# RMS norms of a 512-token network: the sums and the inverse root taken with tokens on the partitions

## What is computed

```python
def rmsnorm(x, g):
    xf = x.astype(jnp.float32)
    y = xf * lax.rsqrt(jnp.mean(xf * xf, axis=-1, keepdims=True) + EPS)
    return (y * g.astype(jnp.float32)).astype(x.dtype)
...
x = x + jnp.concatenate([mix, mem_o], axis=-1) @ w_out
x = x + conv_glu_ffn(rmsnorm(x, g_ffn[i]), f_w_up[i], f_conv_w[i], f_conv_b[i], f_w_down[i])
...
h = modulate(rmsnorm_2(x, g_pre1[l]), sh1, sc1)     # h * (1 + sc1) + sh1
...
x = x + gt1 * rmsnorm_2(y, g_post1[l])
```

## Time and profile before

| | us |
|---|---|
| median of 3 runs | 2332.74 |
| lowest and highest run | 2330.17, 2342.95 |
| the profiled execution, first to last instruction (span) | 2328.2 |
| PE busy | 2129.7 |
| DVE busy | 1305.7 |
| POOL busy | 736.1 |
| ACT busy | 693.4 |

### The profile page before, as it was taken

One profiled execution on the slowest core, in us unless ns is written; L12 is line 12 of the kernel. 1 busy time (PEld: TensorE's weight loads), 2 busy tenths in 40 slices (PEclk: granted clock), 3 DMA queues, 4 the chain that ended last, 5 costly groups with the idle time before them and its releaser, 6 DMA issues.

```text
span 2328.2 us, 25743 instructions
## 1 busy us (share of the span) xinstructions
PE 2129.7 (91%) x9632; PEld 1646.4 (71%) x9632; DVE 1305.7 (56%) x2164; ACT 693.4 (30%) x1099; POOL 736.1 (32%) x181
## 2 busy tenths in 40 slices
PE   6889989899999977898999999679999987999996
PEld 4765567688778864566888888467776665888885
DVE  5878886633953776767336435374433357322336
ACT  4312364322122124552221222223434313212221
POOL 2422102344434431113344443121211232444432
PEclk8989799999999988899999999699999998999998
DMA  4221001422532521003325323121111121223221
GB/s 166 91 73 54 23 1 46 140 102 83 204 135 79 183 94 45 24 24 108 125 74 206 109 87 106 61 79 66 38 55 37 55 91 53 92 75 115 92 83 68
DMA packets 31485, 200.18 MB, mean 86 GB/s; under 512 B 3488, under 2 KB 3616, under 8 KB 13344
## 3 DMA queue, kind: packets, MB, share of 16 engines
q1 hardware_dynamic: 26496, 164.64, 20.6%
q10 hardware_dynamic: 4896, 34.30, 3.9%
HBM read 196.82 MB, written 2.10 MB: 85 GB/s over the span
## 4 chain that ended last, share of the span: by engine, by line
PE 50%; DVE 5%; ACT 1%; issue 0%; POOL 0%; ACTq 0%; DVEq 0%
PE psum L1253 42%; PE psum L1379 2%; PE psum L1410 2%; PE psum L1275 1%; PE psum L1625 1%; DVE work L889 1%; PE psum L1392 1%; DVE work L868 1%; PE psum L1356 1%; DVE h_lo L872 1%; DVE xT L884 0%; DVE work L878 0%; DVE work L893 0%; DVE stats L940 0%; PE psum L1612 0%
## 5 line engine op out<-in xcount | busy, mean ns | idle before, releaser
L509 POOL TENSOR_TENSOR w_lo<-raw,w_hi 128x2048 fp32r<-128x2048 f32 (+2 forms) x176 | 735.7, 4181 | 1561.0 <-ACT w_hi L526 1561.0
L1253 PE MATMUL psum<-h_hi,w_hi 128*128 128x512 f32 x1560 | 623.7, 400 | 11.6 <-POOL w_lo L509 10.1
L1253 PE MATMUL psum<-h_lo,w_hi 128*128 128x512 f32 x1560 | 619.0, 397 | 0.0
L1253 PE MATMUL psum<-h_hi,w_lo 128*128 128x512 f32 x1560 | 618.7, 397 | 0.0
L526 ACT ACTIVATE w_hi<-raw 128x2048 fp32r<-128x2048 f32 (+2 forms) x176 | 301.0, 1710 | 585.4 <-PE psum L1253 479.0
L1253 PEld LDWEIGHTS psum<-h_hi,w_hi 128*128 128x128 f32 x1560 | 297.9, 191 | 91.1 <-issue 20.1
L1253 PEld LDWEIGHTS psum<-h_hi,w_lo 128*128 128x128 f32 x1560 | 297.4, 191 | 74.1 <-issue 12.6
L1253 PEld LDWEIGHTS psum<-h_lo,w_hi 128*128 128x128 f32 x1560 | 298.1, 191 | 72.0 <-issue 12.7
L1253 PE MATMUL psum<-g_hi,w_hi 128*128 128x512 f32 x528 | 206.6, 391 | 8.0 <-issue 5.0
L1253 PE MATMUL psum<-g_hi,w_lo 128*128 128x512 f32 x528 | 205.5, 389 | 0.0
L1253 PE MATMUL psum<-g_lo,w_hi 128*128 128x512 f32 x528 | 205.5, 389 | 0.0
(11 more groups left out here) (240 smaller groups left out, 2710.4 us busy)
## 6 DMA issues: line engine op xcount, KB each, us to landing
raw<-w_up SPq DMA_DIRECT2D x66, 1024.0 KB, 4.8
raw<-w_dn SPq DMA_DIRECT2D x48, 704.0 KB, 4.0
mod_w<-w_mod ACTq DMA_DIRECT2D x24, 1024.0 KB, 5.6
raw<-w_c_in SPq DMA_DIRECT2D x13, 1024.0 KB, 4.9
raw<-w_a_in SPq DMA_DIRECT2D x11, 1024.0 KB, 4.9
raw<-w_b_in SPq DMA_DIRECT2D x7, 1024.0 KB, 4.8
raw<-w_a_out SPq DMA_DIRECT2D x8, 640.0 KB, 3.9
raw<-w_b_out SPq DMA_DIRECT2D x8, 640.0 KB, 3.9
```

The costliest lines, as they stand in the source:

```text
L509: nc.gpsimd.tensor_tensor(LO[slot][:, 0:ph.size], RAW[slot][:, 0:ph.size], HI[slot][:, 0:ph.size].bitcast(F32), ALU.subtract).then_inc(lo_ ...
L1253: ins = nc.tensor.matmul(out, l, r, start=(k == 0 and m == 0), stop=(k == n - 1 and m == 2))
```

## The change

In eleven of the twelve norms (all but ckv) the operands of the summing matmuls change places: 128 tokens of squares are the stationary operand and one column of the ones matrix is the moving one, so the sums of 128 tokens land on 128 partitions in one column. A norm of 512 tokens has 4 such tiles, and each one is a matmul with its own weight load. The root and the reciprocal are then 128x4 (128x2 for 256 tokens), into the new tiles `ROOT` and `INV`. PE lays the inverse out again: for every tile of tokens the column of `INV`, broadcast to 128 columns, is the stationary operand and the identity is the moving one, which leaves the inverse of all tokens on all partitions in bank 4 (bank 3 for mem). DVE's scaling reads it from PSUM in place of `T[:, 3]`. Two semaphores are added, `inverse_ready` (DVE to PE) and `inverse_spread` (PE to DVE). Norms that are not in `SPREAD` keep the sums of the tiles in four banks, 4 to 7. Bank 4 now stays taken until the last chunk has been scaled: `last_read[4]` becomes `scaled_ready` or `x_ready` in place of `root_ready`.

```diff
--- before.py
+++ after.py
@@ -301,6 +301,7 @@
         CST, PRM, ONES = after("const", [NCONST]), after("params", [NPARAM]), after("ones", [P])
         MODV, DER = after("mod", [48, 2]), after("derived", [5, 8])
         ST, M8, WARM = after("stats", [2, 12]), after("top8", [8]), after("tables_warm", [16])
+        ROOT, INV = after("roots", [ROWT]), after("inverses", [ROWT])
 
         CKX, CVX = at("ctx_k", 32, [MEM]), at("ctx_v", 33, [2, P])
         CK, CV = at("c_k", 34, [S]), at("c_v", 52, [ROWT, P])
@@ -342,15 +343,29 @@
                 ("mem", 8, MEM, True), ("mix0", 8, S, True), ("ckv", 2, S, True), ("ffn0", 8, S, True),
                 ("mix1", 8, S, True), ("ffn1", 8, S, True), ("final", 8, S, False), ("ctx", 8, MEM, True),
                 ("pre1", 8, S, True), ("post1", 8, S, False), ("pre2", 8, S, True), ("post2", 8, S, False)]):
-            NORMS[name] = (i, nch, rows, nb, sc)
+            NORMS[name] = (i, nch, rows, nb, sc if splits else None)
             nb += 1 if name in SPREAD else nch
             sc += nch if splits else 0
         square_ready, square_used, root_ready = sem("square_ready"), sem("square_used"), sem("root_ready")
         sum_ready = sem("sum_ready")
+        inverse_ready, inverse_spread = sem("inverse_ready"), sem("inverse_spread")
         scaled_ready, h_hi_ready, h_ready = sem("scaled_ready"), sem("h_hi_ready"), sem("h_ready")
         x_ready = sem("x_ready")
         XR = {"final": 0, "post1": 8, "post2": 16}
 
+
+        def token_sums(name):
+
+            n = NORMS[name][2] // P
+            if name in SPREAD:
+                return bank(4, 0, n)
+            return ps[:, 4 * S:8 * S].rearrange("p (t n) -> p t n", n=S)[:, 0:n, 0]
+
+        ORDER_N = list(NORMS)
+
+        def spread_count(name):
+
+            return sum(n != "ckv" for n in ORDER_N[:ORDER_N.index(name) + 1])
 
         steps, flushes = [], []
 
@@ -559,7 +574,11 @@
 
                     nc.scalar.activation(WARM[:, i:i + 1], cst("eps"), ACT.Sqrt)
                 act.wait_ge(square_used, b + (1 if name in SPREAD else nch))
-                nc.scalar.activation(T[:, 2, 0:rows], bank(4, 0, rows), ACT.Sqrt, bias=cst("eps"),
+                if name == "ckv":
+                    dst_r, sums = T[:, 2, :], bank(4)
+                else:
+                    dst_r, sums = ROOT[:, 0:rows // P], token_sums(name)
+                nc.scalar.activation(dst_r, sums, ACT.Sqrt, bias=cst("eps"),
                                      scale=1.0 / width).then_inc(root_ready, 1)
                 if after_root:
                     after_root()
@@ -865,7 +884,13 @@
             def norm(name, src, gain, shift=None, dst=(HH, HL), into=None):
                 i, nch, rows, b, s = NORMS[name]
                 v.wait_ge(root_ready, i + 1)
-                step(nc.vector.reciprocal(T[:, 3, 0:rows], T[:, 2, 0:rows]))
+                if name == "ckv":
+                    step(nc.vector.reciprocal(T[:, 3, 0:rows], T[:, 2, 0:rows]))
+                    inv = T[:, 3, 0:rows]
+                else:
+                    nc.vector.reciprocal(INV[:, 0:rows // P], ROOT[:, 0:rows // P]).then_inc(inverse_ready, 1)
+                    v.wait_ge(inverse_spread, spread_count(name))
+                    inv = bank(3 if name == "mem" else 4, 0, rows)
 
                 def low(k):
                     v.wait_ge(h_hi_ready, s + k + 1)
@@ -875,7 +900,7 @@
                 for k in range(nch):
                     if into is not None:
                         out = src(k) if into == "self" else T[:, 4 + k % 2, 0:rows]
-                        ins = nc.vector.scalar_tensor_tensor(out=out, in0=src(k), scalar=gain(k), in1=T[:, 3, 0:rows],
+                        ins = nc.vector.scalar_tensor_tensor(out=out, in0=src(k), scalar=gain(k), in1=inv,
                                                              op0=ALU.mult, op1=ALU.mult)
                         if into == "self":
                             ins.then_inc(x_ready, 1)
@@ -886,7 +911,7 @@
                     t = T[:, 4 + k % 2, 0:rows]
                     if k >= 2:
                         v.wait_ge(h_ready, s + k - 1)
-                    ins = nc.vector.scalar_tensor_tensor(out=t, in0=src(k), scalar=gain(k), in1=T[:, 3, 0:rows],
+                    ins = nc.vector.scalar_tensor_tensor(out=t, in0=src(k), scalar=gain(k), in1=inv,
                                                          op0=ALU.mult, op1=ALU.mult)
                     if shift is not None:
                         step(ins)
@@ -1346,16 +1371,45 @@
             def norm(name):
                 i, nch, rows, b, s = NORMS[name]
                 bank_free(4)
+                if name == "ckv":
+                    for k in range(nch):
+                        pe.wait_ge(square_ready, b + k + 1)
+                        nc.tensor.matmul(bank(4, 0, rows), ONES[:], T[:, k % 2, 0:rows], start=(k == 0),
+                                         stop=(k == nch - 1)).then_inc(square_used, 1)
+                    last_read[4] = (root_ready, i + 1)
+                    return
+                tiles = range(rows // P)
                 if name in SPREAD:
                     pe.wait_ge(sum_ready, SPREAD.index(name) + 1)
-                    nc.tensor.matmul(bank(4), ONES[:], T[:, 3, :], start=True, stop=False)
                     pe.wait_ge(square_ready, b + 1)
-                    nc.tensor.matmul(bank(4), ONES[:], T[:, 1, :], start=False, stop=True).then_inc(square_used, 1)
-                for k in range(0 if name in SPREAD else nch):
-                    pe.wait_ge(square_ready, b + k + 1)
-                    nc.tensor.matmul(bank(4, 0, rows), ONES[:], T[:, k % 2, 0:rows], start=(k == 0),
-                                     stop=(k == nch - 1)).then_inc(square_used, 1)
-                last_read[4] = (root_ready, i + 1)
+                    for t in tiles:
+                        nc.tensor.matmul(bank(4, t, t + 1), T[:, 3, t * P:(t + 1) * P], ONES[:, 0:1], start=True, stop=False)
+                        ins = nc.tensor.matmul(bank(4, t, t + 1), T[:, 1, t * P:(t + 1) * P], ONES[:, 0:1], start=False, stop=True)
+                    ins.then_inc(square_used, 1)
+                else:
+                    for t in tiles[1:]:
+                        bank_free(4 + t)
+                    for k in range(nch):
+                        pe.wait_ge(square_ready, b + k + 1)
+                        for t in tiles:
+                            ins = nc.tensor.matmul(bank(4 + t, 0, 1), T[:, k % 2, t * P:(t + 1) * P], ONES[:, 0:1],
+                                                   start=(k == 0), stop=(k == nch - 1))
+                        ins.then_inc(square_used, 1)
+                    for t in tiles[1:]:
+                        last_read[4 + t] = (root_ready, i + 1)
+                pe.wait_ge(inverse_ready, spread_count(name))
+                b = 4
+                if name == "mem":
+                    b = 3
+                    last_read[4] = (root_ready, i + 1)
+                for t in tiles:
+                    ins = nc.tensor.matmul(bank(b, t * P, (t + 1) * P), INV[:, t:t + 1].broadcast_to([P, P]), cst("ident", P),
+                                           start=True, stop=True)
+                ins.then_inc(inverse_spread, 1)
+                if s is not None:
+                    last_read[b] = (scaled_ready, s + nch)
+                else:
+                    last_read[4] = (x_ready, XR[name] + nch)
 
             def h_chunk(name):
                 s = NORMS[name][4]
@@ -1527,7 +1581,7 @@
                 unit_ready(ph, u)
                 b = (u % 2) * 2
                 if u == 1:
-                    last_read[4] = (root_ready, NORMS["mix1"][0] + 1)
+                    last_read[4] = (scaled_ready, NORMS["mix1"][4] + DC)
                     advance(r_tiles(ph, u, range(4), range(4, 8), 0, 256))
                     for t in range(4):
                         last_read[4 + t] = (qkv_ready, 11 + t + 1)
@@ -1578,7 +1632,7 @@
                 if u == 2:
                     advance(t_tiles(ph, u, (0,), (0,)))
                     last_read[0] = (ph.free, 5)
-                    last_read[4] = (root_ready, NORMS["pre1"][0] + 1)
+                    last_read[4] = (scaled_ready, NORMS["pre1"][4] + DC)
                     advance(r_tiles(ph, u, range(4), range(4, 8), P, P))
                     for t in range(4):
                         last_read[4 + t] = (qkv_ready, 17 + t + 1)
```

## The result

The changed kernel takes 2365.27 us (median of 4 runs, 2357.30 to 2371.16) where the kernel before took 2331.45 beside it (2322.94 to 2342.95). The recorded ratio, which is not simply that of the medians, is 1.0123, interval 1.008 to 1.0165. By the medians the change costs 34 us. The forecast was +8.8, and the new median lies above the prediction's range, which ended at 2356. The profiled execution took 2360.68 us, its span is 2358.6, 30.4 more than before; its granted clock has a mean of 0.933, where before had 0.947.

A forecast was written before the change was run, and what follows sets the result against it. PE was taken as the bound, busy 2129.7 of 2328.2 us. Terms -2.1 - 0.3 - 3.0 + 2.95 + 9.65 + 1.6 = +8.8 us gave a median of 2341.5, range 2327 to 2356.

The forecast's parts named there:

- largest term: Between post1 and pre2: the held bank 4 delays pre2's sums until post1's last addition, +9.65 us.
- same: Whole kernel: time within 0.5% or 11.7 us of the kernel before; chance 0.58.
- Passes: Norm sums: one moving column is spaced as 128 are, 0.11 us at clock 1.00 and 0.21 at 0.50.
- rival 2: Every sum and inverse: passes spaced by the load's whole record, 0.33 us at 0.50; +33.5, 2375 us; chance 0.10.
- pre1: Norm pre1: all sums at clock 0.50 make the root 3.9 us later; net +2.95 us.
- rival 1: Norm sums: the clock comes up and passes take 0.11 us; sum -5.5, time 2327.3 us; chance 0.15.
- post1 and pre2: pre2's sums wait for bank 4 until post1's last addition; root +10.6, less 0.95, net +9.65 us.
- Root to PE: Wait from root to PE's restart: 7.3 us for 9.2 in ffn0, 9.1 for 10.05 in pre1.
- rival 4: ffn0, mix1, ffn1: chunk 0's h_lo gets in before POOL's pass, 10 us won, 2332 us; chance 0.05.
- the SPREAD norms at clock 1.00: SPREAD norms: 16 passes behind the last square add 0.85 us, and the inverse takes 1.25, at clock 1.00.
- rival 3: Behind the norms the clock stays low longer; half of ten resumptions give +8.5, 2350 us; chance 0.14.
- The start: Start, with mem and mix0: later weight copy and colder PE against faster scalings, net +1.6 us, from -1.6 to +5.

The follow-up runs named there:

- w_wide_ones: warm_index with 128 columns of ones instead of one in the sums of mem, mix0, ctx, pre1 and pre2: 2324.90 us, ratio 0.9932.
- own_bank: The changed kernel with post1's inverse moved to bank 3: 2350.12 us, ratio 1.007.
- w_late_split: w_spread_only with the second weight copy and POOL's split in ffn0, mix1 and ffn1 behind the first two copies of h: 2320.90 us.
- w_best: w_spread_only with the seven-chunk sums of the SPREAD norms ahead of the wait for the last squares: 2309.95 us, ratio 0.9883.
- w_best_wide: w_best with 128 columns of ones as moving operand in the six SPREAD norms: 2307.53 us, ratio 0.9876.
- w_spread_only: warm_index with the old norm in mem, mix0, ctx, pre1 and pre2, and post1's inverse in bank 3: 2320.71 us, ratio 0.9903.
- start_old: The changed kernel with the old sums and reciprocal in mem and mix0: 2350.30 us, ratio 1.0069.
- w_all_wide: warm_index with post1's inverse in bank 3, seven-chunk sums ahead of the last wait, and 128 columns of ones everywhere: 2310.36 us, ratio 0.9879.
- warm_index: The changed kernel with 32 unused 512-column matmuls while PE waits for the first index queries: 2340.69 us, ratio 1.0025.
- again: The changed kernel run and profiled once more without any edit: 2355.93 us, ratio 1.012.

## Why the prediction was wrong

The direction of its sum was right, and so was its largest term; its size was not, and the "same" that it gave the best chance did not come. By its own steps:

- **Passes.** 64 in 13.9 us at 0.50 were forecast, 13.81 and 13.78 measured. One moving column is spaced as 128 are: rival 2 falls. The forecast that narrow sums do not raise the clock held in pre1 and pre2, against rival 1. The Trainium skill (TensorE: Matmul & The Clock Gate, What's actually happening) has activity release the throttle; the trace does not agree for these passes, with PE busy for 13.8 us at 0.50, and agrees for the 128-column ones of w_wide_ones.
- **pre1.** +3.2 for +2.95. **post1 and pre2.** +11.2 for +9.65, by the mechanism named; own_bank shows 9.0 of it. The rest is post1, which was to end 1.5 earlier and ended 0.4 later (see the step that failed).
- **Root to PE.** 7.34 and 8.84 us for 7.3 and 9.1; POOL's cover is as forecast, rival 4 falls, and w_late_split shows what it hides.
- **The step that failed: the SPREAD norms at clock 1.00.** I priced 16 passes at +0.85 and the inverse at 1.25 us, "at 1.00". The clock falls in this place: in ffn0, final, post1 and post2 it drops within the 16 passes. From the start of the last square to the root (us, the profiles of before and after):

| | ffn0 | mix1 | ffn1 | final | post1 | post2 |
|---|---|---|---|---|---|---|
| before | 1.91 | 2.86 | 1.91 | 1.91 | 1.91 | 1.91 |
| after | 4.04 | 4.42 | 2.79 | 3.92 | 3.83 | 3.50 |
| difference | +2.1 | +1.6 | +0.9 | +2.0 | +1.9 | +1.6 |
| forecast | +0.85 | +1.6 | +0.85 | +0.85 | +0.85 | +0.85 |

The lines of post2 before, and in the changed kernel:

```profile
2308.55 0.69 DVE L993 TENSOR_TENSOR work<-y 128x512 f32<-128x512 f32 x1
...
2310.46 0.69 ACT L562 ACTIVATE work<-psum,const 128x512 f32<-128x512 f32 x1 [14.64 <-PE psum L1353]
```

```profile
2338.90 0.69 DVE L1018 TENSOR_TENSOR work<-y 128x512 f32<-128x512 f32 x1
...
2342.40 0.26 ACT L581 ACTIVATE roots<-psum,const 128x4 f32<-128x4 f32 x1 [16.22 <-PE psum L1387]
...
2342.93 2.08 PE L1406 MATMUL psum<-const,inverses 128*128 128x128 f32 x8 [0.57 <-DVE inverses L891]
```

The inverse takes 2.08. So from the root to the first scaling there are 2.64 us for 4.11, a gain of 1.47 where 2.35 were forecast, and the late root eats it. ffn0 +0.1, ffn1 -0.5, final with ctx 0 and post2 +0.1 stand for -5.1 in all, and post1's share is the same miss. w_best and w_best_wide, which differ only in the width of the sums, show that the one-column passes are what lets the clock fall ahead of the inverse. Where the clock stayed up through the sums, the sum's price was right (ffn1, +0.9), but the gain was not whole: PE restarts 1.0 us sooner against its last square in ffn1, and then runs at 0.50 for 4.4 us of its products where it was 3.4 before, so that 0.5 is left. That is the mechanism of rival 3. ffn0 of w_spread_only, with its sums at 1.00 too, brought 0.8 of the forecast 1.05. The earlier trace rows already showed PE idle for 1.48 us ahead of these passes; I took their price from rows of a busy PE.

- **The start.** +2.6 for +1.6, within its bounds. But start_old and w_spread_only, which have the old norms there, keep 1.3 and 1.1 of the loss, so the nearness is partly luck.
- **c_out, +1.5, had no term.** A stretch of 3.4 us at 0.50 (1886.8 to 1890.2 in the changed kernel) stands there, and none before. It is in every trace with one-column sums in pre1, but also in two with wide ones (c_out 45.4 in w_wide_ones and in w_all_wide) and in w_late_split, which has the old ones. The cause is open.
- **The index stage had no term either**, and needed a wider range instead. Its draw gives 11.8 of the 30.4 us between the profiles. It was in sight beforehand: three runs of the same kernel lay 13 us apart.

The sum on a steady clock is 19.1 us, itself with 1.1 of an untouched piece; the medians of the first comparison lie 34 apart. I put the other 15 down to draws of the index stage: the traces have it from 128 to 149 us long, and warm_index, without it, is 15 below again. For single unprofiled runs this is argued, not shown.

## What to carry to other kernels

Before a result is moved into a bank that is read later than before, list who needs that bank next: here one chunk loop's worth of cover (9 us) hung on it, and a spare bank gave it back. Price small matmuls that follow a wait at the low clock, put those that need not wait ahead of the wait, and don't take a one-column matmul for the cheaper one: here it cost as much as 128 columns and left the clock down. When runs of one kernel scatter by more than the effect, find the stage that scatters and steady it first.

## What the runs showed of the hardware that was not expected

- A dense run of fp32 passes with one moving column kept the clock at 0.50 for all of its 13.8 us, in pre1 and pre2 of every trace that has one there; with 128 columns it came up after 29 passes in pre1 and 21 in pre2 of w_wide_ones. The cost of a pass did not depend on the width: 0.213 us at 0.50 and 0.112 at 1.00 for both.
- After one wait of 7 us the index stage ran at 0.50 for 15.4, 15.5, 47.7 or 51.2 us with PE busy throughout (the last in own_bank):

```profile
151.50:202.70 51.20, 51.20 (x100) 28.35 (x100) 17.18 (x30) 7.16 (x15) 4.59 (x1) 0.50 0.12 41
```

The same program showed the first and the third. Filling the wait with 7.42 us of unused matmuls took 15 us off the kernel after, by its median, and its ten runs lie within 8 us.
- DVE's scalings with the inverse in PSUM never took more than 750 ns in the changed kernel (line 914, the 48 of 512 tokens), where the same with both tensors in SBUF reached 5071 before. In ffn0 two of them ran beside POOL's split.
